# One hybrid decoder step: the decode attention and the retention's projections in one program block, a norm chain cut into steps, and 520 columns at the end

## The chip, the cores and the metric

The kernel runs on one core of a Trainium2 chip. The metric is device time of the whole kernel in microseconds (us), the median of several runs. The engines are TensorE (PE, matmuls, with PEld for the weight loads), VectorE (DVE), ScalarE (ACT), GpSimd (POOL) and SyncE (SP, which issues the transfers here). Each has its own instruction queue and they meet at semaphores.

## The reference, cut to what matters

One layer of a decoder with 1024 channels runs over a prompt of 512 tokens behind 16 learned meta tokens, and one new token for each of 8 running sequences. All share the projections: 16 + 512 + 8 = 536 columns.

```python
xn = rms_norm(h, lp['norm_mix'])
rq, rk, rv, rg, qa, ckv, kr, gr, gm = split_cols(xn @ lp['w_in'])
...
def mla_keys(c, kr, w_uk, g_kn):
    k_nope = einsum('bsr,rhd->bshd', c, w_uk)
    return rms_norm(concatenate([k_nope, broadcast(kr)]), g_kn)

def mla_decode(q, c_new, kr_new, pool_c, pool_kr, page_table, lp):
    ...  # per sequence: 32 pages of 128 cached latents c (256 wide) and rotary keys kr (32 wide)
    s = einsum('bqhd,bkhd->bhqk', q, mla_keys(c, kr, ...)) * scale
    p = softmax(s)                      # over 4096 cached tokens and the new one
    lat = einsum('bhqk,bkr->bhqr', p, c)
    return einsum('bhqr,rhd->bqhd', lat, lp['w_uv'])

def finish_layer(h, o_ret, rg, o_mla, gr, gm, lp):
    r = (silu(rg) * rms_norm(o_ret)) @ lp['w_ret_o']
    m = o_mla @ lp['w_mla_o']
    h = h + (sigmoid(gr) * r + sigmoid(gm) * m) @ lp['w_out']
    u = relu(rms_norm(h, lp['norm_ffn']) @ lp['w_up'])
    return h + (u * u) @ lp['w_down']
y_prompt = hp[:, N_META:]               # the 16 meta columns of the layer's output are not returned
```

The meta columns are needed as keys and values and in the retention's state, and nowhere behind the two branches.

## The kernel before

Tokens lie along the free axis: a projection makes one tile of 128 output channels by 536 tokens, as two PSUM banks of 268 columns. Every float32 product is three matmuls (high part by high, high by low, low by high).

The order of the stages is `project_tokens` (to about 117 us), `prompt_attention` (to 228), `decode_attention` (to 725), `project_retention` (to 967), `retention` (to 1087), then `mix_branches` and `feed_forward` in one chain (to the end).

**Chains of projections** (`linear_chain`, L1100 on). A chain is a list of stages (`Linear`), each a loop over pairs of weight tiles. SP loads a tile (512 KB) into `ring.raw[s]`, ACT copies its high part (L1149), DVE subtracts for the low part (L1175), PE runs 48 matmuls (8 blocks x 3 x 2 halves, L1212), and another engine empties PSUM. Two buffers alternate. `project_retention` is a chain of 16 tiles (rq, rk, rv), 8 (rg) and 16 (the gates), emptied at L1302; `mix` has 8 whole and 8 half tiles, `out` 8, and up and down 64 in four stages. The loads of the first two tiles are issued at the start of `decode_attention`, and their high and low parts are made at its end (L825, L938).

**Decode** (`decode_attention`, L603 on). 8 sequences of 32 pages, four pages to a group, eight groups to a sequence. For each page PE makes the keys of 8 heads and the scores at once (12 matmuls of 260 columns, L968; the weights `wq_hi` and `wq_lo` hold the query in 4 of 260 columns, in one half of the buffer for each parity of the sequence). ACT squares them (L772) into one of four buffers and copies the scores (`s_nope`, L773); DVE sums the squares (`sums`, L858); POOL makes the low part of the next latents (L716). ACT's square waits for the sum four pages earlier, and PE's page for ACT's copy two pages earlier. At a group's end DVE adds the rotary scores (`gather`, L864 and L867).

A sequence is closed while the next one runs, by hooks `(g, j)`: after page `j` of group `g`. DVE's `normalize` (L873 to L885: mean squares, the reciprocal root in ten steps L86 to L93, the scores, the max over a partition's keys) stands in one piece ahead of group 0's first `sums`. Then PE turns the max (`turn_max`, L1000, at (1,2)), DVE takes it over partitions, PE spreads it (L1004, at (2,2)), ACT takes exponentials (L779), PE sums the values (`values`, 64 matmuls and two, L992 and L996, at (3,2)), DVE and PE finish (L1010, L1012, at (4,2)). The last sequence is closed after its last page, with nothing beside it, then the output (L1059).

`c_values` has two buffers of 32 pages, by the parity of the sequence. SP issues for each group four loads of keys (L688) and four of values (L695). PE's queue has group 0 and 1 of sequence 0 written out, a loop over its other groups (L1042), a loop of three iterations with two sequences (16 groups) each (L1045), and the last sequence written out; static slices of `wq` are chosen by parity.

Of the kernel before, what the change touches and what calls it, by code (L numbers as in the profile page):

```python
# [20 lines left out]
P = 128  # L21
# [4 lines left out]
NB = 8  # L26
T = NPROMPT + NB
HT = T // 2
TILES = [(t * P, min(P, T - t * P)) for t in range((T + P - 1) // P)]
# [48 lines left out]

RSQRT_STEPS = 9


def rsqrt(dve, y, t, tmp, chain, at, done):
# [520 lines left out]
def decode_attention(nc, m, ps, ring):  # L603
# [3 lines left out]
    p = Plan(nc, m.b0)  # L607
    table = p("page_table", [1, NB * NPG], I32)
    uvr = p("uv_raw2", [P, 2, MH * VD])
    qa = p("q_absorbed", [P, 2, MH, NB])  # L610
    qah, qal = p("qa_hi", [P, 2, MH, NB], F32R), p("qa_lo", [P, 2, MH, NB], F32R)
    qrope = p("q_rope", [P, NB, GP, MH])
    ct = p("ct_raw", [P, 2, GP, KVL + RD])
    krc, kt = p("krope", [P, GP, RD]), p("krope_t", [P, PAGE])
    kr2, kr4 = p("kr_squares", [P, GP, RD]), p("kr_sums", [P, NPG])
    ssq, sn, sraw = p("k_sums", [P, NPG, MH]), p("s_nope", [P, 2, GP, 2, 4]), p("s_raw", [P, NPG, MH])
# [6 lines left out]
    lat = p("latent_t", [P, 2, NB, MH])  # L623
    pall = p("p_pages", [P, NPG, 32])
    wql = p("wq_lo", [P, 2, 2, 2, WQN], F32R)
    cv_at = p.at
    cv = p("c_values", [P, 2, NPG, KVL + 1])
    assert p.at <= m.end, (p.at, m.end)


    p = Plan(nc, cv_at + 4 * NPG * (KVL + 1))
    ukr, ukt = p("uk_raw2", [P, 2, MH * ND]), p("uk_t", [P, MH, KVL])
    p = Plan(nc, m.small)
    wqh = p("wq_hi", [P, 2, 2, 2, WQN], F32R)
    assert p.at <= m.small_end, (p.at, m.small_end)

    p = Plan(nc, m.ring + 2 * 4 * KD * P)
    k2 = p("k_squares", [P, GP, 2, 4, ND])
    cth, ctl = p("ct_hi", [P, GP, KVL], F32R), p("ct_lo", [P, GP, KVL], F32R)
    assert p.at <= m.small  # L640
# [4 lines left out]
    cv_in = sem("p3_cv_in")  # L645
    (kr_done, kr_turned, kt_done, ct_hi, ct_lo, k_done, k_free, sq_done, red_done, kr_sq, kred, chain, y_done, rope_done, rope_free,
     comb_done, wq_done) = (sem("p3_" + x) for x in (
         "kr_done", "kr_turned", "kt_done", "ct_hi", "ct_lo", "k_done", "k_free", "sq_done", "red_done", "kr_sq", "kred", "chain",
# [11 lines left out]

    def of_sequence(w, b):
# [3 lines left out]
    with nc.Block(no_gpsimd_drain=True) as block:  # L665
        @block.sync
        def _(sp):
# [14 lines left out]
            def keys(n, half, pages, first=False):  # L682

# [6 lines left out]
            def values(b, g, pages):  # L690

                for j in range(GP):
                    page = cv[:, bass.ds(b % 2, 1), GP * g + j, 0:KVL] if isinstance(g, int) else \
                        cv[:, bass.ds(b % 2, 1), bass.ds(GP * g + j, 1), 0:KVL].rearrange("p o g r -> p (o g) r")
                    sp.dma_start(page, m.d_c[bass.ds(pages[j], 1)].rearrange("o k r -> k o r")).then_inc(cv_in, 16)  # L695

            for g in range(NGR):
                pages = table_row(g)
                keys(g, g % 2, pages, first=g < 2)
                values(0, g, pages)  # L700
            sp.wait_ge(zeroed, 9)
            sp.wait_ge(ab_done, 1)
            with sp.Fori(1, NB) as b:
                for g in range(NGR):
                    pages = table_row(NGR * b + g)
                    keys(NGR * b + g, g % 2, pages)
                    if g == 0:
                        sp.wait_ge(cv_in, 16 * NPG * b)
                        sp.wait_ge(pv_done, 1 * b)
                    values(b, g, pages)  # L710

        @block.gpsimd
        def _(pool):
# [4 lines left out]
            def group(n, half, first=False):  # L718
# [4 lines left out]
                pool.wait_ge(set_in, 80)  # L723
# [18 lines left out]
        def _(act):  # L742
            act.wait_ge(set_in, 80)
# [1158 lines left out]
```

## Time and profile before

| | us |
|---|---|
| median of 3 runs (1620.57 to 1622.29) | 1620.64 |
| the profiled execution's own time | 1616.67 |
| its span in the profile | 1614.7 |
| mean granted clock of PE, share of full speed | 0.95 |
| PE busy | 1484.0 (92%) |
| DVE, ACT, POOL busy | 792.0, 599.6, 293.8 |

The span runs from the first to the last instruction that the profile shows, 2 us less than the execution's own time. Matmuls are pipelined: a matmul's record lasts longer than the distance to the next one, so paces are read from distances.

### The profile page before, as it was taken

The page shows a single profiled execution, that of the slowest core. Times are in us where ns is not written, and L with a number is a line of the kernel's source. Part 1 is how long each engine was busy: PE and PEld are TensorE (multiplying, and loading weights), DVE is VectorE, ACT ScalarE, POOL GpSimd, SP SyncE. Part 2 cuts the span into 40 slices and gives each one's busy share as a digit, 9 for nine tenths or more (in the row PEclk, how much of TensorE's full clock was granted, in tenths as well). Part 3 has the DMA queues.
Part 4 walks back from the last instruction along what each step waited for, and adds up shares of the span by engine and source line. Part 5 has one row for each costly group of instructions (what it writes and reads, how often), then busy time and mean ns, then how long its engine had stood idle before and what let it go on. Part 6 is the DMA issues. An engine that isn't in the chain of part 4 may idle for free. (4 is left out here: it accounts for less than half of the span.)

```text
span 1614.7 us, 34170 instructions
## 1 busy us (share of the span) xinstructions
PE 1484.0 (92%) x11404; PEld 1386.1 (86%) x11404; DVE 792.0 (49%) x1494; ACT 599.6 (37%) x1487; POOL 293.8 (18%) x481
## 2 busy tenths in 40 slices
PE   7858979999999999969999998869999999999998
PEld 6746659998899899859999995549998999999998
DVE  5664544655664664542334336754455433334444
ACT  3334435655555556531122224322222331133211
POOL 2250005554544454420000000000040000000000
PEclk9978988999999999989999998879999999999999
DMA  5002126555555555512223214423222222222222
GB/s 208 17 10 56 41 84 179 163 155 148 164 151 148 159 159 147 157 38 92 91 92 127 84 55 136 134 92 104 96 78 74 83 91 81 88 92 91 81 103 79
DMA packets 118943, 170.64 MB, mean 106 GB/s; under 512 B 25457, under 2 KB 96146, under 8 KB 118034
## 3 DMA queue, kind: packets, MB, share of 16 engines
q1 hardware_dynamic: 118866, 169.56, 33.4%
q8 instruction: 55, 0.90, 0.2%
q14 instruction: 22, 0.18, 0.0%
HBM read 153.20 MB, written 7.53 MB: 100 GB/s over the span
## 5 line engine op out<-in xcount | busy, mean ns | idle before, releaser
L968 PE MATMUL ps<-wq_hi,ct_hi 128*128 128x260 f32 x1024 | 303.0, 296 | 18.3 <-ACT s_nope L773 11.3
L968 PE MATMUL ps<-wq_lo,ct_hi 128*128 128x260 f32 x1024 | 292.0, 285 | 0.0
L968 PE MATMUL ps<-wq_hi,ct_lo 128*128 128x260 f32 x1024 | 292.0, 285 | 0.0
L1212 PE MATMUL ps<-x_hi,ring_hi 128*128 128x268 f32 x1280 | 266.2, 289 | 11.2 <-DVE ring_lo L1175 9.7
L858 DVE TENSOR_REDUCE k_sums<-k_squares 128x8 f32<-128x512 f32 (+1 forms) x256 | 172.9, 684 | 200.5 <-ACT k_squares L772 200.3
L1212 PE MATMUL ps<-x_lo,ring_hi 128*128 128x268 f32 x1280 | 263.8, 288 | 0.0
L1212 PE MATMUL ps<-x_hi,ring_lo 128*128 128x268 f32 x1280 | 263.3, 287 | 0.0
L716 POOL TENSOR_TENSOR ct_lo<-ct_raw,ct_hi 128x256 fp32r<-128x256 f32 x256 | 189.0, 739 | 355.1 <-ACT ct_hi L765 353.7
L1149 ACT ACTIVATE ring_hi<-ring_raw 128x1024 fp32r<-128x1024 f32 x126 | 129.0, 1024 | 271.0 <-PE ps L1212 229.2
L772 ACT ACTIVATE k_squares<-ps 128x512 f32<-128x512 f32 x256 | 153.0, 598 | 191.8 <-PE ps L968 171.3
L968 PEld LDWEIGHTS ps<-wq_hi,ct_hi 128*128 128x128 f32 x1024 | 195.7, 191 | 22.9 <-issue 22.7
L1212 PEld LDWEIGHTS ps<-x_hi,ring_hi 128*128 128x128 f32 x1280 | 201.9, 190 | 11.6 <-DVE ring_lo L1175 9.8
L1212 PEld LDWEIGHTS ps<-x_lo,ring_hi 128*128 128x128 f32 x1280 | 202.0, 190 | 0.0
L1212 PEld LDWEIGHTS ps<-x_hi,ring_lo 128*128 128x128 f32 x1280 | 200.9, 189 | 0.0
L968 PEld LDWEIGHTS ps<-wq_lo,ct_hi 128*128 128x128 f32 x1024 | 196.0, 191 | 0.0
L968 PEld LDWEIGHTS ps<-wq_hi,ct_lo 128*128 128x128 f32 x1024 | 195.6, 191 | 0.0
L1175 DVE TENSOR_TENSOR ring_lo<-ring_raw,ring_hi 128x1024 fp32r<-128x1024 f32 x126 | 157.2, 1248 | 56.2 <-ACT ring_hi L1149 55.2
L1212 PE MATMUL ps<-u_hi,ring_hi 128*128 128x268 f32 x512 | 106.7, 290 | 4.4 <-DVE u_lo L1711 4.4
L765 ACT ACTIVATE ct_hi<-ct_raw 128x256 fp32r<-128x256 f32 x256 | 107.0, 419 | 0.0
L1212 PE MATMUL ps<-u_lo,ring_hi 128*128 128x268 f32 x512 | 106.1, 289 | 0.0
L1212 PE MATMUL ps<-u_hi,ring_lo 128*128 128x268 f32 x512 | 106.0, 289 | 0.0
L1649 POOL TENSOR_TENSOR h_square_sum<-h_mid 128x536 f32<-128x536 f32 x1 | 1.1, 1081 | 471.9 <-DVE h_mid L1631 471.9
(291 smaller groups left out, 2131.8 us busy)
## 6 DMA issues: line engine op xcount, KB each, us to landing
ct_raw<-in_ct SPq DMA_DIRECT2D x256, 144.0 KB, 2.3
c_values<-in_c SPq DMA_DIRECT2D x256, 128.0 KB, 2.4
ring_raw<-in_wmain SPq DMA_DIRECT2D x40, 512.0 KB, 3.2
ring_raw<-in_up SPq DMA_DIRECT2D x32, 512.0 KB, 3.2
ring_raw<-in_down SPq DMA_DIRECT2D x32, 512.0 KB, 3.3
state_new<-in_state SPq DMA_DIRECT2D x4, 1024.0 KB
out_st_s<-state_new SPq DMA_DIRECT2D x4, 1024.0 KB, 4.5
ring_raw<-in_reto SPq DMA_DIRECT2D x8, 512.0 KB, 3.3
```

The lines of the kernel that those rows point to most:

```text
L716: nc.gpsimd.tensor_tensor(ctl[:, j, :], ct[:, half, j, 0:KVL], cth[:, j, :].bitcast(F32), ALU.subtract).then_inc(ct_lo, 1)
L765: nc.scalar.activation(cth[:, j, :], ct[:, half, j, 0:KVL], ACT.Copy).then_inc(ct_hi, 1)
L772: nc.scalar.activation(k2[:, j].rearrange("p b h d -> p b (h d)"), d[:, :, 0:4 * ND], ACT.Square).then_inc(sq_done, 1)
L858: dve.tensor_reduce(to, k2[:, j].rearrange("p b h d -> p (b h) d"), AX.X, ALU.add).then_inc(red_done, 1)
L968: mm = nc.tensor.matmul(k_ps[j % 2][:, f, 0:WQN], ch[:, j, r * P:(r + 1) * P], w[:, x2, r, f, :], start=(r == 0 and x == 0), stop=(r == 1 ...
L1149: nc.scalar.activation(ring.hi[s][:, 0:nk, :], ring.raw[s][:, 0:nk, :], ACT.Copy).then_inc(ring.hi_done, 1)
L1175: nc.vector.tensor_tensor(ring.lo[s][:, 0:nk, :], ring.raw[s][:, 0:nk, :], ring.hi[s][:, 0:nk, :].bitcast(F32), ALU.subtract).then_inc(rin ...
L1212: mm = nc.tensor.matmul(ps[s][:, b, 0:HT], w[:, k, :], x[:, k, b * HT:(b + 1) * HT], start=(k == 0 and j == 0), stop=(k == nk - 1 and j == 2))
L1649: nc.gpsimd.tensor_tensor(mid(m.h_sq[:]), of, of, ALU.mult).then_inc(sq_sum, 1)
```

## The change

1. The chain of projections becomes a class `Chain` with one method for each engine, so that `decode_attention` can run the chain of `project_retention` inside its own program block. The first four pairs of the chain are written out (`lead`) and call a hook behind each tile, where the close of the last sequence stands. The high and low parts of the first two weight tiles are made ahead of groups 6 and 7 of the last sequence. The uv weights, used by the output matmuls alone, are loaded at the end instead of at the start.
2. The norm chain is cut: a beginning (`norms`) ahead of group 0, then one step (`refine`) behind each of the eight sums of groups 0 and 1. The max and all later hooks move one group back. `s_raw` gets a second buffer.
3. `c_values` has one buffer. Groups 0 to 2 of a sequence's values are loaded at its groups 6 and 7, groups 3 to 7 at the next sequence's groups 0 to 3.
4. PE's loop runs over one sequence (sequences 1 to 7, eight groups each, so six taken branches) and takes the half of `wq` by register.
5. The clearing of `p_pages` moves from the head of DVE's queue to behind the low part of q, and ACT's first placing of q waits for it.
6. From rg and the gates on, only columns 16 to 535 are computed: 2 x 260 instead of 2 x 268, in mix, out, up and down too; the output `y` has 520 columns.

```diff
+FT = T - N_META
+HF = FT // 2
...
+def rsqrt_step(dve, i, y, t, tmp, chain, at, done):
+    if i == 0:
+        dve.tensor_scalar(y.bitcast(I32), t.bitcast(I32), -0.5, float(0x5F3759DF), ALU.mult, ALU.add).then_inc(chain, 1)
+        return
+    dve.wait_ge(chain, at + i)
+    if i % 3 == 1:
+        dve.scalar_tensor_tensor(tmp, y, -0.5, y, ALU.mult, ALU.mult).then_inc(chain, 1)
+    elif i % 3 == 2:
+        dve.tensor_tensor(tmp, tmp, t, ALU.mult).then_inc(chain, 1)
+    else:
+        dve.scalar_tensor_tensor(y, tmp, 1.5, y, ALU.add, ALU.mult).then_inc(done if i == 9 else chain, 1)
...
+    EARLIER, OWN = {0: (3,), 1: (4,), 2: (5,), 3: (6, 7)}, {6: (0,), 7: (1, 2)}
...
-            sp.dma_start(uvr[:], m.d_uv).then_inc(set_in, 16)
-            sp.wait_ge(set_in, 80)
+            sp.wait_ge(set_in, 64)
...
+            def values(b, g):
+                pages = table_row(NGR * b + g)
+                if g == 0 and not isinstance(b, int):
+                    sp.wait_ge(pv_done, b + 1)
...
             with sp.Fori(1, NB) as b:
                 for g in range(NGR):
+                    keys(NGR * b + g, g % 2)
+                    for v in EARLIER.get(g, ()):
+                        values(b - 1, v)
+                    for v in OWN.get(g, ()):
+                        values(b, v)
+            for g in EARLIER:
+                for v in EARLIER[g]:
+                    values(NB - 1, v)
+            sp.wait_ge(kr_sq, NB * NGR)
+            sp.dma_start(uvr[:], m.d_uv).then_inc(uv_in, 16)
+            chain.sync(sp)
...
             for g in range(NGR):
+                if g >= NGR - 2:
+                    chain.first_hi(act, g % 2)
                 group(b, g, g % 2, closes=True, final=(g == NGR - 1))
+            def close(i, s):
+                if (i, s) == (1, 0):
+                    exp(b)
+                if (i, s) == (2, 0):
+                    take_acc(b)
+            chain.scalar(act, close)
...
-            dve.memset(pall[:], 0.0).then_inc(zeroed, 1)
...
+            dve.wait_ge(zeroed, 8)
+            dve.memset(pall[:], 0.0).then_inc(zeroed, 1)
...
                 if closes and g == 0:
-                    normalize(b - 1)
+                    norms(b - 1)
                 for j in range(GP):
                     sums(n, g, j)
+                    if closes and g < 2:
+                        refine(b - 1, *((0, 1), (2,), (3,), (4,), (5,), (6,), (7,), (8, 9))[GP * g + j])
+                    if closes and (g, j) == (2, 0):
+                        normalize(b - 1)
+                    if closes and (g, j) == (2, 1):
+                        max_of_keys(b - 1)
-                    if closes and (g, j) == (1, 2):
+                    if closes and (g, j) == (2, 3):
                         max_of_heads(b - 1)
...
-                    if closes and (g, j) == (1, 2):
+                    if closes and (g, j) == (2, 2):
                         turn_max(b - 1)
-                    if closes and (g, j) == (2, 2):
+                    if closes and (g, j) == (3, 2):
                         spread_max(b - 1)
-                    if closes and (g, j) == (3, 2):
-                        values(b - 1, 1 - x2)
                     if closes and (g, j) == (4, 2):
+                        values(b - 1)
+                    if closes and (g, j) == (5, 2):
                         finish(b - 1)
...
-            with pe.Fori(0, NB // 2 - 1) as twice:
-                for x2 in (1, 0):
-                    for g in range(NGR):
-                        group(2 * twice + 2 - x2, x2, g, g % 2, closes=True)
+            with pe.Fori(1, NB) as b:
+                for g in range(NGR):
+                    group(b, g, g % 2, closes=True)
...
+            def close(i, s):
+                if (i, s) == (0, 1):
+                    turn_max(b)
+                if (i, s) == (1, 0):
+                    spread_max(b)
+                if (i, s) == (2, 0):
+                    values(b)
+                if (i, s) == (3, 0):
+                    finish(b)
+                if (i, s) == (3, 1):
+                    output()
+            chain.tensor(pe, (k_free, NPG * NB), close)
...
-                                mm = nc.tensor.matmul(ps[s][:, b, 0:HT], w[:, k, :], x[:, k, b * HT:(b + 1) * HT],
+                nk, skip, half = stage.blocks[s], stage.skip, (T - stage.skip) // 2
+                            mm = nc.tensor.matmul(ps[s][:, b, 0:half], w[:, k, :], x[:, k, skip + b * half:skip + (b + 1) * half],
...
+    return Chain(nc, ps, ring, [stage(0, 16), stage(16, 8, rg_sigmoid, rg_silu, skip=N_META),
+                                stage(24, 16, gate, rotate_first, first_head, skip=N_META)], ahead=True, lead=4)
...
+    chain = project_retention(nc, m, ps, ring)
     with nc.cleanup_on_exit():
         prompt_attention(nc, m, ps)
-        decode_attention(nc, m, ps, ring)
-    project_retention(nc, m, ps, ring)
+        decode_attention(nc, m, ps, ring, chain)
```

The bodies of `Chain`'s methods are those of `linear_chain` but for the hooks, `lead`, `first_hi`, `first_lo` and `skip`. `normalize` of the new code holds the scores alone, `norms` and `refine` the steps ahead of it, `max_of_keys` the max behind it.

## Rows read from the trace of the kernel before

**Rows 1.** The page, busy time, share of the span and instructions of each engine.

```profile
PE 1484.0 (92%) x11404; PEld 1386.1 (86%) x11404; DVE 792.0 (49%) x1494; ACT 599.6 (37%) x1487; POOL 293.8 (18%) x481
```

**Rows 2.** Windows by stage: busy us of PE, PEld, DVE, ACT, POOL; clock; DMA share.

```profile
228.00:725.00 497.00, 457.46 (x3932) 434.87 (x3932) 270.82 (x576) 273.21 (x903) 229.05 (x384) 0.96 0.51 150
725.00:967.00 242.00, 239.13 (x1920) 238.95 (x1920) 84.88 (x92) 54.80 (x63) 0.00 (x0) 0.99 0.26 90
...
1087.00:1614.00 527.00, 511.11 (x4036) 509.63 (x4036) 230.28 (x251) 136.24 (x167) 20.97 (x15) 0.98 0.26 90
```

**Rows 3.** Waits of PE: us in total, times, longest.

```profile
PE ps L968 <- ACT s_nope L773: 11.3, 5, 2.3
...
PE ps L954 <- DMA uv_raw<-in_uv: 4.6, 1, 4.6
...
PE ps L968 <- POOL ct_lo L716: 4.1, 2, 2.3
...
PE ps L968 <- issue: 2.9, 1, 2.9
```

**Rows 4.** Pace: PE timeline in decode; the emptying of ten 536-column tiles.

```profile
661.17 0.28 PE L968 MATMUL ps<-wq_hi,ct_lo 128*128 128x260 f32 x1
...
664.04 0.28 PE L968 MATMUL ps<-wq_hi,ct_lo 128*128 128x260 f32 x1
...
L1302 DVE TENSOR_TENSOR z<-ps,rms_x x10: 715/716/718, 745.7 to 799.2; 128x536 f32 x10
```

**Rows 5.** Timeline of PE at the end of decode.

```profile
703.49 0.28 PE L968 MATMUL ps<-wq_hi,ct_lo 128*128 128x260 f32 x1
711.70 0.38 PE L1000 MATMUL ps<-consts,max_part 128*8 128x128 f32 x1 [7.93 <-DVE max_part L885]
...
714.31 5.89 PE L992 MATMUL ps<-c_values,p_pages 128*32 128x257 f32 x64 [1.02 <-issue]
...
726.24 0.78 PE L1212 MATMUL ps<-x_hi,ring_hi 128*128 128x268 f32 x2 [1.51 <-PEq L1794]
...
728.61 0.63 PE L1212 MATMUL ps<-x_hi,ring_lo 128*128 128x268 f32 x2
```

**Rows 6.** Timeline of DVE at the end of decode.

```profile
704.43 0.69 DVE L858 TENSOR_REDUCE k_sums<-k_squares 128x8 f32<-128x512 f32 x1 [0.98 <-ACT k_squares L772]
...
711.02 0.62 DVE L885 TENSOR_REDUCE max_part<-scores 128x8 f32<-128x264 f32 x1
```

**Rows 7.** Timeline of PE, values of a sequence amid decode.

```profile
325.34 3.67 PE L992 MATMUL ps<-c_values,p_pages 128*32 128x257 f32 x64
```

**Rows 8.** Windows, two sequences of decode, from finish to finish.

```profile
335.95:393.23 57.28, 54.82 (x483) 52.17 (x484) 33.21 (x69) 33.51 (x113) 28.66 (x48) 1.00 0.53 157
...
451.16:509.92 58.76, 56.30 (x484) 53.65 (x484) 33.21 (x69) 33.50 (x113) 28.64 (x48) 0.97 0.52 153
```

**Rows 9.** Timeline of DVE at the start of decode.

```profile
229.36 0.91 DVE L831 MEMSET p_pages<- 128x1024 f32 x1 [0.16 <-issue]
```

**Rows 10.** Timeline of DVE, steps of the norm chain and the sums behind.

```profile
650.86 0.84 DVE L93 SCALAR_TENSOR_TENSOR ch_y<-ch_u,ch_y 128x256 f32<-128x256 f32 x1
651.74 0.42 DVE L89 SCALAR_TENSOR_TENSOR ch_u<-ch_y 128x256 f32<-128x256 f32 x1
...
656.50 2.46 DVE L858 TENSOR_REDUCE k_sums<-k_squares 128x8 f32<-128x512 f32 x4
```

**Rows 11.** Branches of PE's loops: duration in ns, least, median, most.

```profile
L1045 PEldq COMPARE_BRANCH  x3: 83/3412/4032, 412.4 to 645.1; - x3
...
L520 PEldq COMPARE_BRANCH  x4: 76/213/243, 152.4 to 228.3; - x4
```

**Rows 12.** Timeline of PE behind a stall.

```profile
483.77 0.42 PE L968 MATMUL ps<-wq_lo,ct_hi 128*128 128x260 f32 x1
```

**Rows 13.** Timeline of SP in decode.

```profile
399.48 1.90 SPq L688 DMA_DIRECT2D ct_raw<-in_ct  x4
```

**Rows 14.** Register operations of the scoring matmul with a register address.

```profile
L982 PEldq FUSED_REGOPS  x6: 46/51/51, 302.2 to 592.3; - x6
```

More of the change, by code:

```diff
@@ L1099, in __init__ @@
         self.sp_start, self.act_start, self.dve_start, self.pe_start = sp_start, act_start, dve_start, pe_start
[L1100 to L1112 removed]
+        self.sp_pair, self.by_act, self.skip = sp_pair, by_act, skip
@@ new lines, in sync @@
+    def sync(self, sp):
+        ring = self.ring
+        if not self.ahead:
+            for s in range(2):
+                self.fetch(sp, self.stages[0], 0, s, self.start + s)
+        for stage, after in self.each():
+            if stage.sp_start:
+                stage.sp_start(sp)
+            with sp.Fori(1, stage.pairs) as i:
+                for s in range(2):
+                    self.fetch(sp, stage, i, s, ring.base + 2 * i + s)
+                if stage.sp_pair:
+                    stage.sp_pair(sp, i)
+            if after:
+                for s in range(2):
+                    self.fetch(sp, after, 0, s, ring.base + 2 * stage.pairs + s)
+        if self.sp_end:
+            self.sp_end(sp)
@@ new lines, in scalar, with pair @@
+    def scalar(self, act, more=None):
+        def pair(stage, i, later):
+            for s in range(2):
+                if stage.act_evac:
+                    stage.act_evac(act, i, s)
+                if later:
+                    self.hi(act, later, i + 1, s)
+                if more and stage is self.stages[0] and isinstance(i, int) and i < self.lead:
+                    more(i, s)
+        if not self.ahead:
+            for s in range(2):
+                self.first_hi(act, s)
+        for stage, after in self.each():
+            if stage.act_start:
+                stage.act_start(act)
+            lead = self.lead if stage is self.stages[0] else 1
+            for i in range(lead):
+                pair(stage, i, stage)
+            with act.Fori(lead, stage.pairs - 1) as i:
+                pair(stage, i, stage)
+            pair(stage, stage.pairs - 1, after)
@@ L1118, in linear_chain, with gpsimd, count @@
+    def gpsimd(self, pool):
+        for stage, after in self.each():
+            if stage.pool_evac:
+                for s in range(2):
+                    stage.pool_evac(pool, 0, s)
+                with pool.Fori(1, stage.pairs) as i:
+                    for s in range(2):
+                        stage.pool_evac(pool, i, s)
+    def count(self):
+        for _ in self.each():
+            pass
+def linear_chain(nc, chain):
     with nc.Block(no_gpsimd_drain=True) as block:
@@ L1158, in _ @@
-            ring.base = start
-            if not ahead:
-                for s in range(2):
-                    split(stages[0], 0, s)
-            for stage, after in each():
-                if stage.act_start:
-                    stage.act_start(act)
-                pair(stage, 0, stage)
-                with act.Fori(1, stage.pairs - 1) as i:
-                    pair(stage, i, stage)
-                pair(stage, stage.pairs - 1, after)
+            chain.scalar(act)
         @block.vector
@@ L1185, in _ @@
-            ring.base = start
-            if not ahead:
-                for s in range(2):
-                    split(stages[0], 0, s)
-            for stage, after in each():
-                if stage.dve_start:
-                    stage.dve_start(dve)
-                pair(stage, 0, stage)
-                with dve.Fori(1, stage.pairs - 1) as i:
-                    pair(stage, i, stage)
-                pair(stage, stage.pairs - 1, after)
+            chain.vector(dve)
         @block.tensor
@@ L1235, in linear_chain @@
-    for _ in each():
-        pass
+            chain.gpsimd(pool)
+    chain.count()
 class Heads:
```

477 lines of the change are left out of this document (237 added, 240 removed).

## The prediction

> **What bounds the kernel now.** I read the page's busy shares first: the matmul engine is busy for 92% of the span, nothing else above half [rows 1]. So only two things change the time: fewer or shorter matmuls, and fewer gaps between them. The windows by stage tell which of the two is left where [rows 2]: the two stretches of projections are busy for 99% and 97%, so only shorter matmuls help there; the decode stretch has some 40 us of idle time in 497. The chain of waits of PE says what ends those gaps [rows 3]: ScalarE's copies of a page's scores five times, POOL's low halves and "issue" once each inside the loop, the uv load at the start. ScalarE is only the last link of the five: it waits for VectorE's sums, and they wait behind the norm chain (below).
>
> **520 columns (the largest term).** The tiles of rg and of the two gates (24), mix (8 whole and 8 half tiles, worth 12), out (8) and the four feed-forward stages (64) drop from 2 x 268 to 2 x 260 columns: 108 tiles of 48 matmuls, 5184. Both widths are in the trace. In decode, 24 matmuls of 260 columns follow each other in 664.04 - 661.17 = 2.87 us, 119.6 ns each; a tile of 268 columns is emptied every (799.2 - 745.7)/9 = 5.94 us, 123.8 ns each [rows 4]. The difference is 4.2 ns; a mere share of 8/268 would be 3.7. The decode matmul differs in its tensors, so I take 3.7 (3.3, which is 8 columns at 2.4 GHz, to 4.2): 5184 x 3.7 = **-19.2 us** (17 to 22). The shorter operations on the other engines count nothing: they are covered by PE, busy 97% there [rows 2].
>
> **The seam between decode and the projections.** The last page begins its last matmul at 703.49; the first projection matmul starts at 726.24 [rows 5]. Between them stands the close of the last sequence, link by link: VectorE's sums from 704.43 and the norm chain to the max at 711.02 [rows 6], turned on PE at 711.70, values from 714.31, output matmuls, then 1.51 us for the end of one program block and the start of the next. From the last page's end (703.8) that is 22.4 us. The first ten projection matmuls then take 2.37 us (726.24 to 728.61) instead of 1.24 by [rows 4], half the pace, which is the lower clock level, 1.2 GHz, after a stretch of idling: about 1.2 us more. In the new program PE goes from the last page to tile (0,0), and turn, spread, values, finish and output sit behind tiles (0,1), (1,0), (2,0), (3,0), (3,1). Two tiles are 11.5 us, more than the norm chain's 7.2 (704.43 to 711.64), and each later hook has a tile or more (5.7 us) for its few VectorE or ScalarE steps, so none waits. What stays is PE's own work: values at the full clock 3.67 us, as in mid-decode [rows 7], and the small matmuls, some 3.2 us at most. The split of the first two weight tiles moves before groups 6 and 7 of the last sequence; ScalarE and VectorE are busy 33.5 and 33 of 57 us there [rows 8], so about 1 us each is hidden, and I charge 0.5 us as cover may be thin in one place. The reload of the first two weight tiles and uv queue on SP after the last keys; the first is needed two tiles later, 11 us. Sum: -22.4 - 1.2 + 3.7 + 3.2 + 0.5 = **-16 us** (13 to 18).
>
> **The start of decode.** PE, ScalarE and POOL wait for five loads, the last of them uv, 4.6 us of which PE feels [rows 3]. Four remain, in front of it on the same queue; the gain lies between nothing (one of them is as late) and the whole 4.6 (all have long landed). No row says when they land; I take the middle, 2.4. The clearing of p_pages, 0.91 us [rows 9], moves to where ScalarE's placing of q waits for it: +0.9. Sum **-1.5 us** (-2.5 to -0.5).
>
> **Inside decode, what goes.** The seven closings run the norm chain in one piece at the head of the next sequence's group 0. VectorE then catches up with four sums in one go at 656.50 [rows 10], and PE stands 2.26 us in five of the seven. In the other two, PE stands for 2.90 and 2.28 us [rows 3]; these fall with the two taken branches of the loop at L1045, which last 3.4 to 4.0 us, against 0.2 us for those of the prompt's loop [rows 11]. After three of the stalls the granted clock fell: 0.42 us instead of 0.28 for a matmul at 483.77 [rows 12], and a sequence with the fall lasts 58.8 us at a mean clock of 0.97, one without it 57.3 at 1.00 [rows 8]: 1.5 us each. Sum 11.3 + 2.9 + 2.3 + 3 x 1.5 = **-21 us**.
>
> With single steps between sums a step costs a sum 0.43 us of delay, up to 0.84 beside POOL [rows 10]; sum and step together take 1.1 to 1.5 us, and a page is 12 x 119.6 ns = 1.44. VectorE stays about level, and ScalarE reads a buffer four pages old, so no page waits. The split costs a few more semaphore waits on VectorE, hidden the same way.
>
> **Inside decode, what is late next.** The turn of the max now stands behind page 2 of group 2, and the max behind the sum of page 1. From the end of a page to the end of its sum is 1.35 us (703.77 to 705.12, [rows 5, 6]); the max adds 0.62 and the chain's lag on VectorE, by the 0.84 us steps, 0.4 to 0.8: 2.4 to 2.8 us after the end of page 1. PE is there after one more page and small matmuls, 1.44 + 0.3 = 1.7 (55.0 us of a sequence without its stall, less 32 pages and the values, leaves 0.65 a group for everything small, of which I take half). So PE waits some 1.1 us in each of seven sequences, **+7.7 us** (0.3 to 1.6 each, 2 to 11); the pages behind it wait with it, but ScalarE and POOL gain what it loses. The later hooks (spread, values, finish) have a full group of four pages each, as now.
>
> **Values held once.** Their loads move: groups 0 to 2 at the end of their own sequence, the rest at the first four groups of the next. Group 0 waits until the values of the sequence before are read (group 4), two groups earlier. In two groups SP issues twelve transfers instead of eight, each about 0.48 us (four in 1.90) [rows 13], some 6 us of a group's 6.9 (55.0/8): tight, but keys are loaded a group ahead. I charge nothing; if that cover is gone it is about a transfer per such group, 0.5 us x 14 = 7 us, and that I leave inside the range.
>
> **The loop over sequences.** Six taken branches of eight groups take the place of two of sixteen, and the weights are addressed by register. The one matmul of the loop that has such an address now, one in each group, takes six register operations of about 50 ns in three iterations of sixteen groups [rows 14]: the address is worked out once per sequence. I cost it at nothing, in the shadow of a queue that issues small matmuls twice as fast as these run (64 in 3.67 us, 57 ns each) [rows 7]. For the branch both ends stand in [rows 11]: 0.2 us, or the 3.4 to 4.0 us of which PE feels 2.3 to 2.9. The old body has 768 page matmuls and the weight loads, the new one half; the prompt's loop, smaller again, is free. On a scale of size the new body lies midway. I take the free end, since a body that is held at all is held whole, and keep the other end as a rival.
>
> **The sum.** -19.2 - 16 - 1.5 - 21 + 7.7 = -50 us. The profiled execution took 1616.67 us, 2 us more than its span; it becomes 1566.7. The median of the runs shown lies 4 us above that execution, so **1571 us** for the median. Ends: best -22 - 18 - 2.5 - 19 gives 1560, worst without a rival -17 - 13 - 0.5 - 10 gives 1580.
>
> **Rivals.**
> *The branch stays dear* (28%). Each of six taken branches stops PE for 2.3 to 2.9 us: +15.6, **1587 us**. For it: nothing but size tells the dear loop from the cheap one [rows 11]. Against: the body is halved.
> The Trainium skill, "Runtime: NRT & Kernel Launch", section "Instruction fetch mechanics", says that a taken branch to a target outside the two pages of instructions then held forces a fetch before execution goes on. By that rule the new branch would be dear too and the time this rival's, 1587 us; the two dear branches of the trace agree with it, and no row shows how much is held.
>
> *VectorE falls behind* (8%). If steps and sums together pass a page's time, PE still stands in every sequence, 2.26 us x 7 on top of the waits for the max: about +12, **1583 us**. For it: the 0.84 us steps [rows 10]; against: only those beside POOL are that long.
>
> *The columns give nothing* (4%): if something other than columns set the pace, -19 is lost, **1590 us**. Against it, the two paces of [rows 4].
>
> *Register addresses slow the matmuls* (4%, the other side). 7 sequences x 32 pages x 12 = 2688 matmuls. If each needs an address operation of its own that PE's queue can't hide, 25 ns each is +67 us: **1638 us**, slower than before. It decides from 50/2688 = 18.6 ns each. Against: one operation per sequence now [rows 14].
>
> The forecast itself (1560 to 1580) has 56%. The range **1560 to 1590** takes in the branch and VectorE. A measurement of this kernel can tell about 0.2%, 3 us: faster 0.94, within 0.02, slower 0.04.
>
> **What would show it.** Tiles of 24 of the 40, and all later ones, emptied every 5.75 to 5.77 us; PE without a gap between the last page and L1212's successor, values among the tiles; no wait of PE for ScalarE's s_nope, but seven of about 1 us for the max before the transposing matmul; branches of the sequence loop at 0.2 us. The prediction is wrong if those branches last over 2 us, if decode's matmuls of 260 columns come slower than 119.6 ns, if the waits for the max pass 2 us and take the clock down, or if the keys come late behind the values.

## The result, and the profile after

The changed kernel takes 1652.64 us (median of 4 runs, 1647.1 to 1655.86) against 1620.61 before (4 runs, 1616.29 to 1622.29): 1.0198 times as long, 95% interval 1.0164 to 1.0233. The forecast was 1571 us, in 1560 to 1590, with 0.94 on faster. It is slower, by 32 us, and the slowest run before (1622.29) lies 25 us under the fastest run after (1647.1). No rival named the cause; the last of the prediction's signs of being wrong did, "if the keys come late behind the values", but it had no price.

The profiled execution took 1647.1 us. Its page begins:

```profile
span 1645.0 us, 34828 instructions
...
PE 1480.2 (90%) x11404; PEld 1378.1 (84%) x11404; DVE 788.7 (48%) x1493; ACT 600.0 (36%) x1487; POOL 298.3 (18%) x481
```

PE's busy time fell by 4 us [rows 1] while the span grew by 30. Windows of the changed kernel, with columns as in [rows 2]: one sequence of decode, then part of the projections, then mix to the end.

```profile
365.40:433.10 67.70, 59.53 (x483) 56.33 (x482) 33.21 (x69) 33.53 (x113) 28.86 (x49) 0.92 0.45 131
840.00:1000.00 160.00, 160.00 (x1332) 160.00 (x1331) 58.42 (x63) 40.28 (x48) 0.00 (x0) 1.00 0.31 101
1142.80:1644.30 501.50, 485.92 (x4036) 484.53 (x4036) 227.43 (x251) 135.16 (x167) 20.37 (x15) 0.99 0.28 93
```

A sequence of decode lasts 67.7 us where it took 57.3 to 58.8 [rows 8], at a clock of 0.92 instead of 0.97 to 1.00. The projections are as tight as they were, and from mix to the end the same 4036 matmuls take 501.5 us in place of 527 [rows 2]. So the loss lies in decode. What PE waits for, in the changed kernel:

```profile
PE ps L1037 <- ACT krope_t L823: 55.7, 23, 4.2
...
PE ps L1292 <- DVE ring_lo L1200: 16.3, 2, 10.2
...
PE ps L1009 <- DMA c_new_rows<-out_ckv_s: 4.5, 1, 4.5
```

The five waits for `s_nope` are gone, as forecast, and so is the wait of 7.9 us for the last max. In their place PE waits 23 times, 55.7 us, in front of the matmul of the rotary scores. That one needs the turned rotary keys, which ACT copies. ACT's own waits, in the changed kernel, say why they are late:

```profile
ACT ct_hi L788 <- DMA ct_raw<-in_ct: 59.5, 23, 4.4
```

ACT waits for the keys themselves (`ct_raw`): 59.5 us, 23 times. ACT's waits in the kernel before have no such line. In ACT's queue the high part of the next group's first page (`ct_hi`) stands ahead of the copy of the turned rotary keys, and ACT comes to the copy only when that page has landed (timeline of ACT):

```profile
464.48 0.42 ACT L788 ACTIVATE ct_hi<-ct_raw 128x256 fp32r<-128x256 f32 x1 [4.31 <-DMA ct_raw<-in_ct]
464.81 0.26 ACT L823 ACTIVATE krope_t<-ps 128x128 f32<-128x128 f32 x1
```

So late keys of the next group stop PE in this one. The timeline of PE shows the same stall, in the middle of a sequence:

```profile
460.75 0.28 PE L1023 MATMUL ps<-wq_hi,ct_lo 128*128 x1
465.12 0.64 PE L1037 MATMUL ps<-q_rope,krope_t 128*128 x2 [4.09 <-ACT krope_t L823]
...
466.59 0.42 PE L1023 MATMUL ps<-wq_lo,ct_hi 128*128 x1
```

4.09 us without work, and behind it matmuls at 0.42 us instead of 0.28: the clock has fallen to its lower level (granted 0.50 from 465.2 to 470.0, 0.98 from 460 to 465). A stall is paid twice.

The keys are issued by SP. Its timeline, in the same sequence (x4 are the four pages of a group; a row joins issues that follow each other, reads of the table included):

```profile
420.10 5.32 SPq L715 DMA_DIRECT2D c_values<-in_c  x8
430.22 1.91 SPq L708 DMA_DIRECT2D ct_raw<-in_ct  x4
433.79 1.88 SPq L715 DMA_DIRECT2D c_values<-in_c  x4
437.31 1.88 SPq L708 DMA_DIRECT2D ct_raw<-in_ct  x4
...
455.23 5.40 SPq L715 DMA_DIRECT2D c_values<-in_c  x8
462.27 13.75 SPq L708 DMA_DIRECT2D ct_raw<-in_ct  x12
```

The row of twelve keys is groups 4 to 6, where SP waits for POOL, since only two groups of keys fit; elsewhere it hardly rests, and yet the keys are late: the first of the twelve is issued at 462.27, and it lands 2.2 us later (the median for keys), when ACT's wait above ends. Four transfers take 1.9 us, as before [rows 13]; but from the end of the keys (432.13) to the first transfer of the values (433.79) pass 1.66 us, and the same again before the next keys. In the kernel before, values followed keys at once, and a reading stood only between a group's values and the next keys; keys end at 401.38 in the group of [rows 13], values begin at 401.60 (timeline of SP, kernel before):

```profile
401.60 2.01 SPq L695 DMA_DIRECT2D c_values<-in_c  x4
...
408.44 2.02 SPq L695 DMA_DIRECT2D c_values<-in_c  x4
412.11 1.90 SPq L688 DMA_DIRECT2D ct_raw<-in_ct  x4
```

What stands in the gap is the reading of four page numbers from the table. Before, one reading served a group's keys and its values. Now the values belong to another group than the keys beside them, so each reads its own row. The line of `table_row` in the kernel before, then in the changed one:

```profile
L679 SPq SEQ_ASSERT  x256: 18/18/37, 237.8 to 688.1; - x128
L679 SPq TENSOR_LOAD <-page_table x64: 295/298/532, 237.0 to 686.8; - x64
```

```profile
L699 SPq SEQ_ASSERT  x512: 18/18/37, 236.6 to 782.1; - x171
L699 SPq TENSOR_LOAD <-page_table x128: 295/298/517, 235.8 to 780.8; - x128
```

128 readings of four numbers instead of 64, 512 bounds checks instead of 256. A group with one load of values now costs SP 7.1 us (430.22 to 437.31), and one with two costs 10.6; PE needs 6.9. Only groups 4 and 5 have no values. Eight readings and transfers of each kind make 8 x 7.1 = 57 us of SP in a sequence of which PE needs 55.

One more thing stops SP in the changed kernel. The values of the row at 420.10 end at 425.42, and the next keys begin at 430.22, 4.8 us later instead of 1.64: there SP's loop over sequences turns (its branch, L721):

```profile
L721 SPq COMPARE_BRANCH  x1: 53/53/53, 425.5 to 425.5; - x1
L721 SPq FUSED_REGOPS  x1: 68/68/68, 428.0 to 428.0; - x1
```

Between the branch and the next instruction lie 2.4 to 2.6 us at each of the six turns. In the kernel before and in the unchecked kernel below it is 0.23 to 0.26 us. The second readings with their checks lengthen the loop: 353 recorded instructions of SP from turn to turn, 277 before, 289 unchecked. A sequence of 67.9 us is then, on SP, some 57 us of readings and transfers, 2.3 us more at the turn, and the waits inside the six turns of the loop (waits of SP, window 365.4 to 772.7), 6.8 and 1.3 us a sequence:

```profile
SPq L708 <- POOL kr_squares L756: 40.9, 12, 4.9
SPq L715 <- PE ps L1051: 7.7, 6, 1.3
```

### The profile page after: what moved, and what is told of

Read it like the earlier page. It is cut to its first block and busy times, and to the rows that moved or that the text cites. A ratio compares the mean times of both kernels' runs of the same rounds, so it can differ in the third digit from the quotient of the medians.

```text
span 1645.0 us, 34828 instructions
## 1 busy us (share of the span) xinstructions
PE 1480.2 (90%) x11404; PEld 1378.1 (84%) x11404; DVE 788.7 (48%) x1493; ACT 600.0 (36%) x1487; POOL 298.3 (18%) x481
## 5 line engine op out<-in xcount | busy, mean ns | idle before, releaser
L1023 PE MATMUL ps<-wq_hi,ct_hi 128*128 (+1 forms) x1024 | 314.5, 307 | 4.2 <-POOL ct_lo L739 4.2
L1023 PE MATMUL ps<-wq_lo,ct_hi 128*128 (+1 forms) x1024 | 302.5, 295 | 0.0
L1023 PE MATMUL ps<-wq_hi,ct_lo 128*128 (+1 forms) x1024 | 301.9, 295 | 0.0
L1292 PE MATMUL ps<-x_hi,ring_hi 128*128 128x260 f32 (+1 forms) x1280 | 260.1, 284 | 16.3 <-DVE ring_lo L1200 16.3
L1292 PE MATMUL ps<-x_lo,ring_hi 128*128 128x260 f32 (+1 forms) x1280 | 259.9, 285 | 0.0
L1292 PE MATMUL ps<-x_hi,ring_lo 128*128 128x260 f32 (+1 forms) x1280 | 258.9, 284 | 0.0
L1195 ACT ACTIVATE ring_hi<-ring_raw 128x1024 fp32r<-128x1024 f32 (+1 forms) x128 | 131.1, 1025 | 262.4 <-PE ps L1292 201.8
L1200 DVE TENSOR_TENSOR ring_lo<-ring_raw,ring_hi 128x1024 fp32r<-128x1024 f32 (+1 forms) x128 | 159.3, 1245 | 70.3 <-ACT ring_hi L1195 68.8
L788 ACT ACTIVATE ct_hi<-ct_raw 128x256 fp32r<-128x256 f32 x256 | 107.2, 420 | 60.8 <-DMA ct_raw<-in_ct 59.5
L1292 PE MATMUL ps<-u_lo,ring_hi 128*128 128x260 f32 x512 | 103.1, 283 | 0.0
L1292 PE MATMUL ps<-u_hi,ring_lo 128*128 128x260 f32 x512 | 102.6, 282 | 0.0
```

The lines of the kernel that those rows point to most:

```text
L788: nc.scalar.activation(cth[:, j, :], ct[:, half, j, 0:KVL], ACT.Copy).then_inc(ct_hi, 1)
L1023: mm = nc.tensor.matmul(k_ps[j % 2][:, f, 0:WQN], ch[:, j, r * P:(r + 1) * P], of_sequence(w, b)[:, r, f, :], start=(r == 0 and x == 0), s ...
L1195: self.nc.scalar.activation(ring.hi[s][:, 0:nk, :], ring.raw[s][:, 0:nk, :], ACT.Copy).then_inc(ring.hi_done, 1)
L1200: self.nc.vector.tensor_tensor(ring.lo[s][:, 0:nk, :], ring.raw[s][:, 0:nk, :], ring.hi[s][:, 0:nk, :].bitcast(F32), ALU.subtract).then_in ...
L1292: mm = nc.tensor.matmul(ps[s][:, b, 0:half], w[:, k, :], x[:, k, skip + b * half:skip + (b + 1) * half], start=(k == 0 and j == 0), stop=( ...
```

## The experiments

Two theories were set against each other. *The queue*: SP's own time sets the pace, and the second reading of rows is what it lacks. *The hold*: the new wait for the single buffer of values, at group 6, holds the keys that stand behind it on SP.

**Same transfers and waits, no second reading** (`keys` returns its registers, so values are loaded from the pages of the group whose keys stand beside them; their own page numbers are left out):

```diff
-            def values(b, g):
-                pages = table_row(NGR * b + g)
+            def values(b, g, pages):
```

> The changed kernel with one thing left out: the four page numbers for a group's values are not read from the page table, the registers just read for that group's keys are used, so the values come from other pages. Transfers, waits and order stay. Queue theory (SP needs 1.66 us to read a row and 1.9 us for four transfers; it now reads 16 rows a sequence instead of 8, and a group with two groups of values takes it 10.5 us against a group of 6.9 on PE, so keys come late): SP needs 44 us a sequence instead of 57, a sequence falls from 67.6 to 55 to 58 us, and the 28 transfers ahead of the first reload of weights shrink too: 1570 to 1585 us. Hold theory (the wait for the last reading of the single values buffer, at group 6, holds the keys behind it on SP): nothing that matters changes, above 1635 us.

1559.59 us, 0.9641 of before (0.9607 to 0.9674). All 64 transfers of a sequence, their order, the doubled groups and the hold are as in the changed kernel; 93 us are gone. The wait of the hold is even longer than the 8.9 us in seven of the changed kernel (waits of SP, in this kernel):

```profile
SPq L715 <- PE ps L1052: 20.3, 7, 2.9
```

The hold falls as the cause. With the readings the long turn of SP's loop is gone too (0.24 us). The gain is larger than expected, as other terms of the prediction were too small (below).

**The second reading without its bounds check**

```diff
-                pages = table_row(NGR * b + g)
+                pages = table_row(NGR * b + g, again="keys() has checked this row")
```

> The changed kernel, with the bounds check left out of the second reading of a row alone (the same row has been read and checked for the keys). Queue theory: a reading falls from 1.66 to some 0.5 us, SP's demand to 48 us a sequence, but the groups with two groups of values still take it 8.5 us: sequences of 57 to 60 us, 1580 to 1605 us. Hold theory: above 1635 us.

1561.79 us, 0.966 (0.9629 to 0.9692). So not even the reading matters, but its checks and what hangs on them. The same rows and the timeline of SP in this kernel:

```profile
L699 SPq SEQ_ASSERT  x256: 18/18/37, 235.8 to 671.7; - x128
L699 SPq TENSOR_LOAD <-page_table x128: 295/299/527, 235.0 to 690.7; - x128
```

```profile
416.22 1.88 SPq L708 DMA_DIRECT2D ct_raw<-in_ct  x4
418.71 1.88 SPq L715 DMA_DIRECT2D c_values<-in_c  x4
422.25 1.88 SPq L708 DMA_DIRECT2D ct_raw<-in_ct  x4
```

128 loads as in the changed kernel, half the checks. From keys (ending at 418.10) to values is 0.61 us instead of 1.66: the check of four numbers is some 1.05 us on SP, the load itself 0.30. A group costs 6.0 us (416.22 to 422.25), less than PE's 6.9. The doubled groups (8.6, from 422.25 to 430.89) are over that, which is why 1580 to 1605 was expected; the two groups of keys that are loaded ahead cover them, a cover that was reckoned too thin. A sequence, and what PE waits for, in this kernel:

```profile
352.80:408.80 56.00, 54.98 (x484) 52.16 (x483) 33.17 (x69) 33.54 (x112) 28.81 (x49) 1.00 0.55 161
```

```profile
PE ps L1009 <- DMA c_new_rows<-out_ckv_s: 4.1, 1, 4.1
PE ps L1055 <- DVE max_part L919: 4.0, 7, 0.6
PE ps L1037 <- ACT krope_t L823: 1.2, 2, 1.0
```

56.0 us at the full clock. In the changed kernel six sequences take (772.7 - 365.4)/6 = 67.9 us each, by the turns of PE's loop (below). So decode gets back 11.9 us a sequence. By the windows of the two kernels some 7 of it are idle time of PE (8.2 us of 67.7 against 1.0 of 56.0), and 4.6 are the same work done faster (59.5 us busy at a clock of 0.92, 55.0 at 1.00). The checks take their own time from SP, 8 x 1.05 = 8.4 us, and with them goes the long turn of SP's loop, 2.3 us; no run has the one without the other in this kernel.

**One load of values in every group, checks as in the changed kernel**

```diff
-    EARLIER, OWN = {0: (3,), 1: (4,), 2: (5,), 3: (6, 7)}, {6: (0,), 7: (1, 2)}
+    EARLIER, OWN = {0: (3,), 1: (4,), 2: (5,), 3: (6,), 4: (7,)}, {5: (0,), 6: (1,), 7: (2,)}
```

> The changed kernel with its values loads spread, one group of values in each group: 3 to 7 in groups 0 to 4 of the next sequence, 0 to 2 in groups 5 to 7 of their own. Rows are read as in the changed kernel, and the wait for the values buffer stands one group earlier. Queue theory: no group costs SP more than 7.2 us, against 6.9 of PE's, so a sequence lasts 57.5 to 60 us and the whole 1585 to 1600 us. Hold theory: the wait comes a group earlier and holds more keys for longer: no faster than now, 1650 us or more.

1628.27 us, 1.0069 (1.0047 to 1.0091): 24 us faster than the changed kernel, against the hold, and 28 to 43 slower than the queue theory said. SP's timeline shows the part that it had missed:

```profile
452.85 1.88 SPq L708 DMA_DIRECT2D ct_raw<-in_ct  x4
456.36 1.88 SPq L715 DMA_DIRECT2D c_values<-in_c  x4
459.88 1.88 SPq L708 DMA_DIRECT2D ct_raw<-in_ct  x4
467.45 1.93 SPq L715 DMA_DIRECT2D c_values<-in_c  x4
```

Groups follow at 7.0 us; but at group 5 the values come 5.7 us after the keys end (461.76 to 467.45), 4.0 us more than a reading. That is the hold, one group earlier than in the changed kernel. Inside the six turns of this kernel's loop SP waits for nothing else (waits of SP, window 363.5 to 745.7):

```profile
SPq L715 <- PE ps L1051: 24.2, 6, 4.2
```

SP has nothing to spare, so here the hold costs its full length, 4.0 us a sequence, and the turn of SP's loop, which stops it for 2.5 to 2.9 us here too, costs the rest: 57 + 4.0 + 2.3 us is a sequence of this kernel, (745.7 - 363.5)/6 = 63.7 us, but for half a microsecond.

**The kernel before, with a second reading**

```diff
                     keys(NGR * b + g, g % 2, pages)
+                    pages = table_row(NGR * b + g)
```

> The kernel before, with each group's row read a second time between its keys and its values; two buffers of values as before. Queue theory: SP's demand rises from 5.5 to 7.2 us a group, 57.3 a sequence, as long as the sequence itself is now (57.1 to 58.8): 0 to 15 us slower, 1621 to 1636, with keys that begin to come late. Hold theory: no single buffer, so no change, within 3 us of before.

1632.46 us, 1.0083 (1.0054 to 1.0113), 13.5 us slower, with the wait of the changed kernel in a program that has nothing else of the change (waits of PE):

```profile
PE ps L983 <- ACT krope_t L801: 15.7, 20, 2.1
```

SP's waits for POOL fall from 66.6 us to 6.3, so SP has become the bound here as well. Its loop still turns in 0.23 us (349 recorded instructions from turn to turn): the reading with its checks does this without a longer turn.

**Spread, unchecked, and the first reload of weights ahead of the last values** (`second` fetches tiles 2 and 3)

```diff
+            chain.second(sp)
             for g in EARLIER:
```

> The unchecked second reading, the spread of the third run, and the first reload of two weight tiles issued ahead of the last sequence's remaining values. Queue theory: with cheap readings SP needs 6 us a group, spread or not, and the hold of 4 us at group 5 fits in what SP has to spare; nothing is left to gain over the unchecked kernel: 1558 to 1566 us. Hold theory in a weaker form (the hold is what cost the spread kernel its gain, checks or not): 7 x 4 us more than the unchecked kernel, some 1590 us.

1566.26 us, 0.9682 (0.9661 to 0.9704). No gain over the unchecked kernel, and nothing near 1590: with time to spare SP takes most of the hold, which lasts 52.6 us in seven here. PE shows eight waits for rotary keys, 3.8 us, which may be what is left of it.

**The max one page later**

```diff
-                    if closes and (g, j) == (2, 2):
+                    if closes and (g, j) == (2, 3):
                         turn_max(b - 1)
```

> The unchecked kernel with PE's turn of the max one page later, behind page 3 of group 2. In the unchecked kernel PE waits seven times 0.57 us, 4.0 us in all, for the max. If that wait is real loss: 4 us faster, 1558 us. If ScalarE's copies and VectorE's sums set the pace of those pages anyway: within 1 us of the unchecked kernel.

1559.99 us, 0.9646 (0.9632 to 0.966), against 0.966 (0.9629 to 0.9692): not to be told from the unchecked kernel. The wait for the max is gone from PE's list, and another has come, in this kernel:

```profile
PE ps L1037 <- ACT krope_t L823: 4.6, 7, 2.4
```

4.6 us for keys behind the doubled groups in place of 4.0 us for the max. The later turn let PE run on until the next thing that was late.

**All 536 columns again**, in the unchecked kernel (and so in every operation behind):

```diff
-FT = T - N_META
+FT = T
...
-    return ap[:, N_META:T]
+    return ap[:, 0:T]
...
-                                stage(24, 16, gate, rotate_first, first_head, skip=N_META)], ahead=True, lead=4)
+                                stage(24, 16, gate, rotate_first, first_head, skip=0)], ahead=True, lead=4)
```

> The unchecked kernel with all 536 columns again from rg and the gates to the end. The prediction's term for the columns: 5184 matmuls by 3.3 to 4.2 ns, 17 to 22 us slower than the unchecked kernel, so 1579 to 1584 us. If the columns gave nothing: 1562 us.

1591.21 us, 0.9829 (0.9811 to 0.9848), 29 us slower than the unchecked kernel, where 17 to 22 were expected. Eleven and ten tiles of the first feed-forward stage, first in the unchecked kernel, then in this one:

```profile
L1818 DVE TENSOR_TENSOR u_sq<-relu x11: 700/701/701, 1199.9 to 1257.0; 128x520 f32<-128x520 f32 x11
```

```profile
L1818 DVE TENSOR_TENSOR u_sq<-relu x10: 716/718/719, 1217.5 to 1270.9; 128x536 f32<-128x536 f32 x10
```

(1257.0 - 1199.9)/10 = 5.71 us a tile against (1270.9 - 1217.5)/9 = 5.93 us: 0.22 us a tile, some 4.65 ns a matmul, 24.1 us for 5184. The rest of the 29 is not in the columns' stages: this kernel's profile is 6.4 us later at the first turn of decode's loop already (359.2 against 352.8), after a prompt attention at a clock of 0.83 instead of 0.92, which the edit does not touch; from there to the end of the two spans (1590.3 and 1558.9) it loses 25.0. Why the prompt ran so in this program stays open.

**No bounds checks at all**, in the unchecked kernel: the keys' readings lose theirs too.

```diff
-            def table_row(n, again=None):
+            def table_row(n, again="left out for the experiment"):
```

> The unchecked kernel with the bounds check left out of the keys' readings too, so that a reading costs SP some 0.6 us everywhere and its demand falls from 6 to 5 us a group. Queue theory: SP is no longer the bound in the unchecked kernel, so nothing more comes of it: within 4 us of it, 1558 to 1563 us. If SP's time still set the pace in part: about 1 us for each of 56 groups, some 1510 us at most, at least clearly below 1555.

1559.01 us, 0.9644 (0.9626 to 0.9661). Another 1 us less of SP in each group brings nothing that can be told, and SP waits longer for POOL instead (115.9 us in place of 49.2): below PE's time, SP's is free.

**One doubled group instead of two**, with the late max

```diff
-    EARLIER, OWN = {0: (3,), 1: (4,), 2: (5,), 3: (6, 7)}, {6: (0,), 7: (1, 2)}
+    EARLIER, OWN = {0: (2,), 1: (3,), 2: (4,), 3: (5, 6), 4: (7,)}, {6: (0,), 7: (1,)}
```

> The kernel with the late max, and with values 0 and 1 loaded at groups 6 and 7 of their own sequence, 2 to 7 at groups 0 to 4 of the next: one group with two loads of values instead of two, and the wait for the buffer stays at group 6. In the late-max kernel PE waits seven times for keys, 4.6 us in all, behind the groups with two loads. Queue theory: that halves, 2 us less than the late-max kernel and some 4 less than the unchecked one, 1557 us. If the hold at group 6 is what makes them late: no change, 1560 us.

1556.27 us, 0.961 (0.9589 to 0.9631): the lowest median of all, 4% below the kernel before. PE waits neither for the max nor for keys in its loop. The unchecked kernel ran beside it:

> The unchecked kernel once more, beside the others of this call: 1562 us as before, 0 to 5 us above the kernel with one doubled group.

1561.46 us, 0.9649 (0.9628 to 0.9671). The 5 us between them fit the expectation, but the intervals overlap by a hair. The traces agree: a turn of PE's loop takes (685.3 - 354.6)/6 = 55.1 us with one doubled group, (687.7 - 351.4)/6 = 56.05 in the unchecked kernel, 6 to 7 us in seven sequences. With the late max alone a turn takes (686.9 - 352.6)/6 = 55.7 us. Each is one profiled execution.

**The kernel before, its one reading unchecked**

```diff
-                                                                min_val=0, max_val=m.pool - 1)[1]
+                                                                min_val=0, max_val=m.pool - 1,
+                                                                skip_runtime_bounds_check_because="left out for the experiment")[1]
```

> The kernel before with the bounds check left out of its one reading of a row for each group. Queue theory: SP needs 5.5 us of a group's 6.9 there and is not the bound, so 1 us less per group changes nothing: within 3 us of before. If reading rows had cost the kernel before too: up to 56 x 1 us less.

1619.15 us, 1.0005 (0.9986 to 1.0024): no change. SP waits longer for POOL instead (137.0 us in place of 66.6). The readings cost the kernel before nothing, at 5.5 us of a group's 6.9.

## Why the prediction was wrong, step by step

**Values held once: the step that failed.** The step reckoned with "twelve transfers instead of eight, each about 0.48 us", together "some 6 us of a group's 6.9", and concluded "I charge nothing; if that cover is gone it is about a transfer per such group, 0.5 us x 14 = 7 us". It counted the transfers that were moved and not what SP executes ahead of each set of them. The reading stood in the diff (`values` got its own `table_row`) and its price in the trace before: from the end of a group's values at 410.46 to the next keys at 412.11 SP issued nothing for 1.65 us. With that the doubled groups come to 10.6 us and a sequence of SP to 57 us, more than the 55 of PE's; measured, a sequence became 67.9 us. Put in, the reading would have named this as the largest rival on the other side. The long turn of SP's loop could not be read from the trace before, where it takes 0.23 us. Without the checks of the second reading the forecast's time is reached and passed: 1561.8 us, in the range. Of the 9 us by which it undercuts the forecast, the terms explain 4: columns gave 5 us more than forecast and the seam 1 more, decode and the start 2 less.

**The seam.** In the unchecked kernel PE goes from the last page to the first tile without a gap (timeline of PE):

```profile
690.74 0.28 PE L1023 MATMUL ps<-wq_hi,ct_lo 128*128 x1
690.86 0.41 PE L1292 MATMUL ps<-x_hi,ring_hi 128*128 128x268 f32 x2
```

and the ninth tile is emptied at 751.46 (timeline of DVE):

```profile
751.46 0.72 DVE L1410 TENSOR_TENSOR z<-ps,rms_x 128x536 f32 x1 [4.83 <-PE ps L1292]
```

From the last page's end (about 691.0) that is 60.5 us; before, the first tile was emptied at 733.75 and the ninth at 781.38, 77.6 us after the last page's end. The first 16 tiles are 536 columns wide in both kernels, so the columns have no part in this. The seam gave 17.1 us (forecast 16). In the changed kernel SP spoilt part of this too: the last sequence's 28 transfers of values with their readings keep the first reload of weights (timelines of SP, then of PE, in the changed kernel):

```profile
757.73 1.88 SPq L708 DMA_DIRECT2D ct_raw<-in_ct  x4
761.16 23.00 SPq L715 DMA_DIRECT2D c_values<-in_c  x28
...
784.97 24.81 SPq L1189 DMA_DIRECT2D ring_raw<-in_wmain  x6
```

```profile
792.89 0.81 PE L1292 MATMUL ps<-x_hi,ring_hi 128*128 128x268 f32 x2 [6.06 <-DVE ring_lo L1200]
```

The reload is issued at 784.97, 27 us after the last keys, and PE waits 6.06 us for the third tile of the chain. The step's "the first is needed two tiles later, 11 us" forgot what stood ahead on the queue. In the unchecked kernel, with the same transfers ahead but short readings, the wait is gone.

**Columns.** Right in kind, too small: 3.7 ns a matmul, 17 to 22 us; measured 4.65 ns, 24 us. The 119.6 ns taken from decode's page matmuls was not the pace of the projections at 260 columns, which is 119.0 (5.71/48), and the difference of the two rows, 4.2 ns, was nearer than the share of 8/268 that I preferred.

**The start.** The first page begins at 245.98 in the unchecked kernel instead of 246.83, 0.9 us earlier (forecast 1.5), but 0.46 of that is a prompt that ended earlier (the first load of decode is issued at 228.35 instead of 228.81). In the changed kernel the first page begins at 246.77, 18.0 us after that load, just as before. PE still waits 4.1 to 4.5 us for loads there, now for `c_new_rows`. The step was worth 0.0 to 0.4 us, less than the low end of its range.

**Inside decode.** The norm chain in steps holds no page: no wait for `s_nope` is left. The wait for the max is real and small: 4.0 us in seven sequences, 0.57 each (forecast 1.1, 0.3 to 1.6; the step's own bounds, 2.4 to 2.8 less 1.7, give 0.7 to 1.1). 56.0 us a sequence stands against 55.0 + 1.1. Over the whole of decode the unchecked kernel gains 11.9 us, where 21 - 7.7 = 13.3 were forecast.

**The loop.** The free end was right. In the changed kernel:

```profile
L1100 PEldq COMPARE_BRANCH  x7: 76/211/224, 365.4 to 772.7; - x7
```

Six taken branches of 0.21 us. The rule of the Trainium skill ("Runtime: NRT & Kernel Launch", "Instruction fetch mechanics") by which they would be dear, with only two pages of instructions held, does not describe this loop; the dear ones of [rows 11] had a body twice as long. Register addresses cost nothing that shows: 56.0 us a sequence leaves no room for it. A dear branch did come, but on SP, whose loop the prediction did not look at.

**Two slips in the working.** The rival in which VectorE falls behind was priced at about 12 us, but 2.26 x 7 is 15.8. And two tiles behind the last page take 11.9 us and not 11.5, as the first 16 tiles keep their 536 columns. Neither bears on the outcome.

**The account.** Spans of the unchecked kernel and before: 1558.9 and 1614.7, 55.8 us apart. The terms as measured: 24.1 + 17.1 + 0.9, and 11.9 in decode (first page to last page's end 445.0 against 456.9), 54.0 us. The changed kernel stands 86.1 us above the unchecked one: 83.1 in decode (528.1 against 445.0) and 7.6 at the seam (from the last page's end to the ninth tile 68.1 against 60.5). That is 4.6 us too much; on the other side stands mainly the retention, whose code the two kernels share: between the projections and mix lie 121.7 us in the changed kernel's profile and 125.5 in the unchecked one's.

The 11.9 us a sequence, as SP's time line has them: 8.4 for eight checks of 1.05 us, 2.3 for the turn of the loop, 2.4 more of waiting for POOL (6.8 against 26.7/6 = 4.4; SP may load only two groups ahead, so a late PE and POOL hold SP again), less 1.3 of the hold (1.3 against 15.3/6 = 2.6). That is a sum of times and not an experiment. What stays open is how much the turn of SP's loop would cost if it stood alone, and why it is long there: no run lengthens the loop without adding work to it.

## What to carry to other kernels

When a change moves transfers between groups, write down for each period everything that the issuing queue executes (reads of indices, bounds checks, address arithmetic, waits, transfers, the turn of its loop), and hold the sum against the period of the engine that it feeds. A queue that is not the bound hides all of that; one that passes the period by a few per cent makes the fastest engine wait, and the wait costs the clock too. A value that two uses shared has a price of its own once the uses are parted; and a check that was made for the first use need not be made again for the second.

## What the runs showed of the hardware that was not expected

- Reading four page numbers into SP's registers takes 0.30 us of load, but 1.66 us with the bounds checks and what surrounds them, 0.61 us without: the checks are two thirds of it.
- A taken branch of PE over 484 matmuls and their weight loads takes 0.21 us, one over 967 took 3.4 to 4.0 us [rows 11].
- SP's loop stood still for 2.4 to 2.9 us behind its branch in the two kernels with 353 recorded instructions of SP from turn to turn, and for 0.22 to 0.28 us in all the others, of which the longest has 349.
- Eight columns fewer of 268 are worth some 4.65 ns, 0.58 ns a column, more than their share of the matmul's pace (3.7 ns of 123.6).
